# A two-block transformer kernel: Strassen's seven products for half of the second FFN's up projection, in turns of 1024 columns

## The reference

```
# first block, D_FF = 5632
h2 = rmsnorm(x, ffn_norm_g)
x = x + (silu(h2 @ w_ffn_gate) * (h2 @ w_ffn_up)) @ w_ffn_down
# second block, D_FF_2 = 8192
h2 = rms_norm(x, g_ff)
x = x + square(relu(h2 @ w_ff1)) @ w_ff2
```

## Time and profile before

| | us |
|---|---|
| median of 3 runs (lowest, highest) | 2602.14 (2601.84, 2602.91) |
| the profiled execution | 2602.48 |
| its span, first to last instruction | 2600.8 |
| TensorE busy | 2589.1 |
| VectorE busy | 1875.7 |
| ScalarE busy | 1400.5 |
| GpSimd busy | 538.1 |
| FFN 1's steady turns | 717 to 1280 |
| FFN 2 from its second panel | 1923 to 2598 |

### The profile page before, as it was taken

The page is one execution under the profiler, slowest core; times in us unless marked ns, Lnnn a source line. Parts: engine busy times, 40 slices in busy tenths (PEclk is TensorE's granted clock), DMA queues, the critical chain, the costliest instruction groups (busy, mean ns, idle before and its releaser), DMA issues.

```text
span 2600.8 us, 34270 instructions
## 1 busy us (share of the span) xinstructions
PE 2589.1 (100%) x11591; PEld 2153.1 (83%) x11591; DVE 1875.7 (72%) x1944; ACT 1400.5 (54%) x1572; POOL 538.1 (21%) x1034
## 2 busy tenths in 40 slices
PE   9999999999999999999999999999999999999999
PEld 8888888888788888888878888888888888888887
DVE  6767788667888888888986655566666666666666
ACT  5546666445555555566555557764454444444443
POOL 2212121232121222222033120003332121212121
PEclk9999999999999999999999999999999999999999
DMA  8666666766588888888787665566766666666664
GB/s 272 212 201 212 210 219 194 251 218 209 187 248 242 243 246 243 245 245 245 251 269 218 200 200 166 180 206 206 227 217 208 201 208 202 208 202 209 201 210 154
DMA packets 305477, 564.61 MB, mean 217 GB/s; under 512 B 28512, under 2 KB 41872, under 8 KB 304880
## 3 DMA queue, kind: packets, MB, share of 16 engines
q1 hardware_dynamic: 261952, 502.25, 59.1%
q0 software_dynamic: 43264, 61.18, 10.5%
q10 hardware_dynamic: 176, 0.07, 0.0%
HBM read 503.75 MB, written 2.10 MB: 194 GB/s over the span
## 4 chain that ended last, share of the span: by engine, by line
PE 91%; PEld 3%; DVE 2%; issue 1%; DMA 1%; SPq 1%; DVEq 1%; POOL 0%; ACT 0%; ACTq 0%; POOLq 0%
PE pair L2339 20%; PE pair L2334 20%; PE pair L2343 20%; PE aux L2339 4%; PE aux L2334 4%; PE aux L2343 4%; PE pair L2623 4%; PE aux L2623 3%; PE aux L2605 2%; PE aux L2608 2%; PE aux L2602 2%; PEld pair L2334 1%; PEld pair L2339 1%; PEld pair L2343 1%; PE pair L2608 1%
## 5 line engine op out<-in xcount | busy, mean ns | idle before, releaser
L1417 DVE TENSOR_TENSOR w_lo<-raw,w_hi 128x1024 fp32r<-128x1024 f32 (+1 forms) x856 | 1026.2, 1216 | 525.2 <-ACT w_hi L808 512.5
L808 ACT ACTIVATE w_hi<-raw 128x1024 fp32r<-128x1024 f32 (+1 forms) x854 | 893.5, 1055 | 905.0 <-PE pair L2343 637.4
L2334 PE MATMUL pair<-w_hi,lhs_hi 128*128 128x512 f32 x1536 | 414.0, 391 | 0.7 <-ACT lhs_hi L860 0.7
L2339 PE MATMUL pair<-w_hi,lhs_lo 128*128 128x512 f32 x1536 | 411.1, 389 | 1.1 <-DVE lhs_lo L1470 1.0
L2343 PE MATMUL pair<-w_lo,lhs_hi 128*128 128x512 f32 x1536 | 411.1, 389 | 0.0
L729 POOL DMA_DIRECT2D arena<-arena x528 | 263.2, 604 | 713.5 <-DVE arena L1921 598.8
L2339 PEld LDWEIGHTS pair<-w_hi,lhs_lo 128*128 128x128 f32 x1536 | 288.2, 188 | 62.2 <-DVE lhs_lo L1470 1.9
L2343 PEld LDWEIGHTS pair<-w_lo,lhs_hi 128*128 128x128 f32 x1536 | 288.0, 188 | 61.0 <-DVE w_lo L1417 1.1
L2334 PEld LDWEIGHTS pair<-w_hi,lhs_hi 128*128 128x128 f32 x1536 | 286.1, 188 | 59.3 <-ACT lhs_hi L860 1.2
L2334 PE MATMUL pair<-w_hi,low_hi 128*128 128x512 f32 (+1 forms) x1048 | 278.3, 387 | 0.0
L2339 PE MATMUL pair<-w_hi,low_lo 128*128 128x512 f32 (+1 forms) x1048 | 277.0, 386 | 0.0
(11 more groups left out here) (341 smaller groups left out, 2881.7 us busy)
## 6 DMA issues: line engine op xcount, KB each, us to landing
raw<-in_w_ff SPq DMA_DIRECT2D x128, 1024.0 KB, 5.2
...
```

The source lines that it names most:

```text
L808: nc.scalar.activation(w_hi[:, at.slot(p, k), :, 0:width], raw[:, at.raw_slot(p, k), 2 * h:2 * h + 2, 0:width], ACT.Copy).then_inc(hi_read ...
L1417: v.tensor_tensor(w_lo[:, at.slot(p, k), :, 0:n], raw[:, at.raw_slot(p, k), 2 * h:2 * h + 2, 0:n], w_hi[:, at.slot(p, k), :, 0:n].bitcast( ...
L2334: nc.tensor.matmul(ps[:, t, 0:n], hi_t[:, ch, tok], w_hi[:, s, c, 0:n], start=start and k == 0 and c == 0, stop=False)
L2339: nc.tensor.matmul(ps[:, t, 0:n], lo_t[:, ch, tok], w_hi[:, s, c, 0:n], start=False, stop=False)
```

## The change

FFN 2 gets FFN 1's form. `ffn2_first` has two ordinary panels of w_ff1 (columns 0 to 1023). Then come TURNS2 = 7 turns (6 in `ffn2`, one in `ffn2_last`), each with 1024 columns of w_ff1 as eight units, four of them by the seven products, and four down panels of 1024 rows (LONG: 8 chunks, 4 granules). A turn gives two groups of 512 hidden columns, so it has two transposes, two moves and two `hid_turn`s, after unit pairs 2 and 6 of the next turn; the second move waits until the first `hid_turn` has been taken, as `move` and its one buffer demand. The results of the last turn's groups go to buffers of their own (`last_hi`, `last_lo`). Down panels are still added by `add_x`, now after the weights of the panel behind. In FFN 1, `hid_turn` stands after unit pair 4 and not 2, and the `t_used` credit is given ahead of `ffn_first`. `move`, `flip`, `recombine`, `seven` and `ordinary` are used as they are.

```diff
+TURNS1 = NB1 - 1
+TURNS2 = NB2 // 2 - 1
+LONG = (8, N)
-    ("ffn2_first", 1, [FULL]),
-    ("ffn2", NB2 - 2, [FULL] + [SHORT] * 4),
-    ("ffn2_last", 1, [FULL] + [SHORT] * 8),
+    ("ffn2_first", 1, [FULL, FULL]),
+    ("ffn2", TURNS2 - 1, [FULL, FULL] + [LONG] * 4),
+    ("ffn2_last", 1, [FULL, FULL] + [LONG] * 8),
...
+            def load_wide_unit(at, u, col):
+                p, k = unit(u)
+                r = at.raw_slot(p, k)
+                sp.wait_ge(lo_ready, at.gran(p, k) + 2)
+                rows = w_ff1_2[0][2 * u * P:(2 * u + 2) * P, bass.ds(col, 2 * N)]
+                sp.dma_start(raw[:, r].rearrange("p (c w) n -> p c (w n)", w=2),
+                             rows.rearrange("(c p) n -> p c n", p=P)).then_inc(raw_loaded[r], 16)
             def ffn2_block(at, i):
-                load(at, 0, w_ff1_2[0], i * N + N)
+                for u in range(8):
+                    load_wide_unit(at, u, i * (2 * N) + 2 * N)
                 for j in range(4):
-                    load(at, 1 + j, w_ff2_2[0], j * N, i * N)
+                    load(at, 2 + j, w_ff2_2[0], j * N, i * (2 * N))
...
@@ scalar, FFN 1
-                    if u == 2:
+                    if u == 4:
                         hid_turn(i)
@@ scalar, FFN 2
             def block2(at, i, last=False):
+                n = i + TURNS1
+                b = i * 2 + NB1
+                for u in (2, 4, 6):
+                    hi_ordinary(at, u, None)
+                    hi_seven(at, u + 1, None)
+                    hi_sums(u + 1, n)
+                    if u == 2:
+                        hid_turn(b, 0, T_FF2 - 1)
+                    if u == 6:
+                        hid_turn(b + 1, 4, T_FF2 - 1)
+                hi(at, 2, 0, 2)
+                act.wait_ge(products, n * 3 + 1)
+                nc.scalar.activation(first_product, aux[:, 0, :], ACT.Copy).then_inc(product_copied, 1)
+                hi(at, 2, 2, 4)
+                act.wait_ge(gates_ready, n + 1)
+                relu_rows(act_f, [gates[:, 1, :], gates[:, 0, :]], b + 2)
+                hi(at, 3, 0, 1)
+                act.wait_ge(hid_ready, b + 4)
+                relu_rows(gates, [hid[:, 0, :], hid[:, 1, :]], b + 3)
+                hi(at, 3, 1, 4)
+                hi(at, 4, 0, 4)
+                if last:
+                    hid_turn(b + 2, 0, T_FF2 - 1, dst=last_hi)
+                hi(at, 5, 0, 4)
+                if last:
+                    hi(at, 6, 0, 2)
+                    hid_turn(b + 3, 4, T_FF2 - 1, dst=last_hi)
+                    hi(at, 6, 2, 4)
+                else:
+                    nxt = At("ffn2", i + 1)
+                    hi_ordinary(nxt, 0, None)
+                    hi_sums(1, n + 1)
+                    hi_seven(nxt, 1, None)
...
             at = At("ffn2_last")
+            block2(at, TURNS2 - 1, True)
+            for j in range(1, 4):
+                hi(at, 6 + j, 0, 4)
@@ vector, FFN 1
                 unit_pair(at, 2, i)
+                unit_pair(at, 4, i)
                 hid_turn(i)
-                unit_pair(at, 4, i)
@@ vector, FFN 2
+            x_norm(5, 18, lambda: s_forms(At("ffn2_first")))
+            lo(at, 1, 2, 4)
             relu_square(at, NB1, pairs[at.pair(0)][:])
+            lo(at, 1, 4, 6)
+            dve.wait_ge(s_hi_ready, 2)
+            v.tensor_tensor(s_lo[:], s_sum[:], s_hi[:].bitcast(F32), ALU.subtract)
+            dve.drain().then_inc(s_ready, 1)
+            lo(at, 1, 6, 8)
+            sums_seven(first, 1, TURNS1, False)
+            lo_ordinary(first, 0)
+            lo_sums(1, TURNS1)
+            lo_blocks(first, 1)
+            relu_square(at, NB1 + 1, pairs[at.pair(1)][:])
             def block2(at, i, last=False):
+                n = i + TURNS1
+                b = i * 2 + NB1
+                unit_pair(at, 2, n, False)
+                hid_turn(b)
+                unit_pair(at, 4, n, False)
+                unit_pair(at, 6, n, False)
+                hid_turn(b + 1, 4)
+                lo(at, 2, 0, 2)
+                recombine(at, n, 0)
+                lo(at, 2, 2, 4)
+                dve.wait_ge(act_ready, b + 3)
+                for t in range(TOK):
+                    v.scalar_tensor_tensor(act_f[:, t, :], gates[:, 1 - t, :], x_inv[:, t:t + 1],
+                                           act_f[:, t, :], ALU.mult, ALU.mult)
+                dve.drain().then_inc(hid_ready, 1)
+                flip(b + (2 + T_FF2), by_chunk(act_f), n_split=1)
+                lo(at, 3, 0, 1)
+                dve.wait_ge(act_ready, b + 4)
+                for t in range(TOK):
+                    v.scalar_tensor_tensor(hid[:, t, :], hid[:, t, :], x_inv[:, t:t + 1],
+                                           gates[:, t, :], ALU.mult, ALU.mult)
+                dve.drain().then_inc(hid_ready, 1)
+                lo(at, 3, 1, 4)
+                add_x(at, 2, 0)
+                lo(at, 4, 0, 4)
+                add_x(at, 3, N)
+                flip(b + (3 + T_FF2), by_chunk(hid), n_split=1)
+                if last:
+                    hid_turn(b + 2, 0, (last_hi, last_lo))
+                lo(at, 5, 0, 4)
+                add_x(at, 4, 2 * N)
+                if last:
+                    lo(at, 6, 0, 2)
+                    hid_turn(b + 3, 4, (last_hi, last_lo))
+                    lo(at, 6, 2, 4)
+                    add_x(at, 5, 3 * N)
+                else:
+                    nxt = At("ffn2", i + 1)
+                    lo_ordinary(nxt, 0)
+                    sums_seven(nxt, 1, n + 1, False)
+                    lo_sums(1, n + 1)
+                    add_x(at, 5, 3 * N)
+                    lo_blocks(nxt, 1)
...
             for j in range(3):
+                lo(at, 7 + j, 0, 4)
+                add_x(at, 6 + j, j * N)
@@ tensor
+            pe.sem_inc(t_used, 2)
             at = At("ffn_first")
...
-            pe.sem_inc(t_used, 2)
             block(At("ffn", 0), 0, True)
...
+            gemm(at, 1, wide)
+            def block2(at, i, first=False):
+                bank_free(at, 0)
+                ordinary(at, 0)
+                bank_free(at, 1)
+                if first:
+                    pe.wait_ge(s_ready, 2)
+                for u in range(1, 8):
+                    if u in SEVEN:
+                        seven(at, u, i + TURNS1)
+                    else:
+                        ordinary(at, u)
+                pe.wait_ge(moved_taken, i * 2 + (NB1 + T_FF2 + 2))
                 for j in range(4):
+                    gemm(at, 2 + j, low)
...
             pe.wait_ge(moved_taken, NB1 + NB2 + T_FF2)
             for j in range(3):
+                gemm(at, 6 + j, (last_hi, last_lo))
+            bank_free(at, 9)
+            pe.wait_ge(lo_ready, at.gran(9, 3) + 1 + LO_CREDIT)
             for n, (t, c0, c1) in enumerate(TAIL):
+                for ch in range(8):
...
```

More of the change, by code:

```diff
@@ L338, in two_blocks @@
     third = aux[:, 2:4, :]
-    tail_bank = [pairs[1][:, 0, :], pairs[1][:, 1, :], aux[:, 0, :]]
+    last_pair = pairs[At("ffn2_last").pair(9)]
+    tail_bank = [last_pair[:, 0, :], last_pair[:, 1, :], aux[:, 0, :]]
     sem = nc.alloc_semaphore
@@ L1108, in _, with hid_turn @@
             squares_of(3, at, 3)
-            def hid_turn(b, c0=0, first=0, split=False):
+            def hid_turn(b, c0=0, first=0, split=False, dst=low_hi):
                 if split:
@@ L1399, in _, with relu_rows @@
-            with act.Fori(0, NB2 - 2) as i:
+            hi(at, 1, 4, 6)
+            act.wait_ge(s_sums_ready, 2)
+            nc.scalar.activation(s_hi[:], s_sum[:], ACT.Copy).then_inc(s_hi_ready, 1)
+            hi(at, 1, 6, 8)
+            hi_ordinary(first, 0, None)
+            hi_sums(1, TURNS1)
+            hi_seven(first, 1, None)
+            gate_function(at, 1, NB1 + 1, ACT.Relu, pairs[at.pair(1)][:])
+            def relu_rows(dst, src, b):
+                for t in range(TOK):
+                    nc.scalar.activation(dst[:, t, :], src[t], ACT.Relu, scale=x_inv[:, t:t + 1])
+                act.drain().then_inc(act_ready, 1)
@@ L1928, in lo_ordinary, with sums_seven @@
                 lo(at, p, k, k + 2)
-            def sums_seven(at, u, i):
+            def sums_seven(at, u, i, halves=True):
                 p, k = unit(u)
@@ L2029, in _, with s_forms @@
             at, first = At("ffn_first"), At("ffn", 0)
-            def s_forms():
+            def s_forms(at):
                 def pairs_of(lhs):
@@ L2047, in s_forms @@
                 dve.drain().then_inc(s_sums_ready, 1)
-            x_norm(3, 11, s_forms)
+            x_norm(3, 11, lambda: s_forms(At("ffn_first")))
             lo(at, 1, 2, 4)
@@ L2290, in relu_square @@
                 flip(b + T_FF2, by_chunk(hid), n_split=1)
-            x_norm(5, 18)
-            lo(at, 0, 8, 12)
+            first = At("ffn2", 0)
+            x_norm(5, 18, lambda: s_forms(At("ffn2_first")))
+            lo(at, 1, 2, 4)
             relu_square(at, NB1, pairs[at.pair(0)][:])
-            def block2(at, i, last=False):
```

(34 more changed lines are left out.)

69 lines of the change are left out of this document (31 added, 38 removed).

## The result

The changed kernel takes **2583.89 us** (median of 6 runs, 2581.58 to 2585.04) beside 2601.99 of the kernel before (6 runs, 2601.36 to 2604.32): a ratio of 0.9927, 95% interval 0.9916 to 0.9937. Forecast were 2583.0 and "faster". The profiled execution took 2585.04, with a span of 2583.3: 17.5 less than before, where 19.4 were forecast.

A forecast was written before the change was run, and what follows sets the result against it. TensorE's count of 512-column matmuls at 0.2267 us each was taken to bound both FFNs. Terms -19.04 + 0.14 - 4.7 + 1.2 + 0.3 + 2.7 = -19.4 us from 2602.5 gave a forecast of 2583, range 2579 to 2591.

The forecast's parts named there:

- The bound and the 84 matmuls: In FFN 2, TensorE's matmul count sets the time; seven turns save 84 matmuls at 0.2267 us each: -19.04 us.
- FFN 1's first turn: TensorE's four stalls in FFN 1's first turn go through the earlier credit and later hid_turn: -4.7 us, bounds -3.1 and -4.7.
- VectorE and ScalarE keep up: In FFN 2's turns of 84.3 us, VectorE is busy 85% and ScalarE some 44 us, so the load fits.
- The edges: Between FFN 2's turns, unit 1's weights come 0.2 us late at each of 6 edges: +1.2 us, bounds 0 and 7.2.
- rival 2: FFN 2's edges cost the whole addition, 1.2 us each, or landing data holds sums_seven: 2589 us, chance 0.15.
- The moves: In FFN 2's steady turns a move takes 12.65 us, and the second may take 18.5 before it costs anything: 0.
- Rival 3: VectorE holds GpSimd's DMAs, a move lasts 24.3 us and TensorE stands before each first down panel: 2624 us, chance 0.04.
- The last turn's second move: In FFN 2's last turn it leaves half a microsecond of slack before TensorE's down panels: +0.3 us, bounds 0 and 3.
- The tail: Before the last panel TensorE idles for its last granule's w_lo: +2.7 us, bounds 2.5 and 2.9.
- Rival 4: The idle before the last panel drops the clock to 1.2 GHz, doubling the following 11.2 us: 2594 us, chance 0.04.
- The sum: Over the whole kernel, all terms together give -19.4 us, from 2602.5 to 2583.1, forecast as 2583 us.

The follow-up runs named there:

- late_turn: The changed kernel with FFN 2's first hid_turn after unit pair 4 instead of 2: 2637.22 us, ratio 1.0131 to the kernel before.
- After_again: The changed kernel itself, unaltered, run again beside the other experiments: 2583.09 us, ratio 0.9924 to the kernel before.
- ffn2_only: The changed kernel with both of FFN 1's edits (credit, hid_turn place) undone: 2589.49 us, ratio 0.9952 to the kernel before.
- edge_sums_first: The changed kernel with VectorE doing unit 1's sums ahead of unit 0's w_lo in FFN 2's turns: 2581.90 us, ratio 0.9922 to the kernel before.
- eight_products: The changed kernel with one product of each seven in FFN 2 computed and added twice: 2601.90 us, ratio 0.9998 to the kernel before.
- Tail_granules: The changed kernel with TensorE waiting for the last panel's weights granule by granule: 2578.46 us, ratio 0.9908 to the kernel before.
- tail_fill: The changed kernel with ten matmuls of unused result run in the wait before the last panel: 2581.99 us, ratio 0.9923 to the kernel before.
- both: The changed kernel with the last panel's granule-by-granule waits and the sums first at FFN 2's edges: 2577.61 us, ratio 0.9904 to the kernel before.

## Why the prediction was right, step by step

**The bound and the 84 matmuls: right.** -19.04 forecast; put back, the turn shows 2.73 us for 12 of them, and the medians 18.8 (20 like with like). The pace in FFN 2's turns is 0.2267.

**FFN 1's first turn: the stalls went as forecast, their cost and their causes were misread.** All four stalls went. The term was -4.7, the sum of the idle in the rows; by the pace the stalls cost 5.7, and the runs gave 5.6. I had given the first to the credit and the three others to the place of hid_turn. The runs say 4.1 us for each alone and 5.6 for both, because the credit moves the whole chain up (sums, transpose, move) and ScalarE's wait with it: the moved blocks came 4.0 us earlier, where the prediction had 1.7.

**VectorE and ScalarE keep up: right.** 85% and 52% as worked out, and no stall inside a turn. The order at the edge was the tight place, as said.

**The edges: right, and 0.07 us each too small.** 0.27 at six edges, 1.6 us, against 1.2. The bound of 7.2 (rival 2) did not come.

**The moves: right.** GpSimd issued 16 DMAs in 7.80 and 7.81 us beside VectorE's dense stretches. From the start of the issue to ScalarE's copy it took 12.4 us in the last turn (2529.74 - 2517.37), where ScalarE was waiting for it; late_turn shows 13.6. The prediction had 12.65 from the transpose's end. All of it fits into 18.5. Late_turn shows that this margin is real: move the first hid_turn by one unit pair and it is overdrawn by 5 us a turn. Rival 3 is out. The rule that rival 3 leaned on was read too widely. The Trainium skill, "SBUF — State Buffer", section "SBUF: two separate sides", says that GpSimd can't write its descriptors while VectorE runs an operation in a 2-port mode; an operation with two SBUF inputs it calls in the way only of GpSimd operations that read SBUF. During the 7.8 us of the steady move VectorE was busy for 7.34, all of it TENSOR_TENSOR operations with two inputs from SBUF, and the 16 DMAs took their usual time: the trace agrees with the page, and no run here shows a 2-port operation beside a move.

**The last turn's second move: 0 instead of 0.3**, with the 0.3 us of slack that the last fence on the moves shows.

**The tail: the gap right, its consequence missed.** 2.72 us by the pace (2.56 of idle) against 2.7. Rival 4 said that the clock would fall behind it and double all of the 11.2 us that follow; I gave it 0.04, because four stalls of up to 1.64 left the clock at 1.00. Its mechanism happened and its size was wrong: seven matmuls at half pace, 1.5 us, then full clock again. After_again, ffn2_only, edge_sums_first and eight_products show it too, with 1.5 to 1.7 us lost; late_turn has the same gap without it. Tail_granules, tail_fill and both, where the gap is gone, never show it. So the standstill is needed and is not always enough; what decides stays open.

**The sum: right within 1 us, in part by luck.** By the pace the terms are -19.04 + 0.14 - 5.7 + 1.6 + 0 + 2.72 + 1.5 = -18.8, against the forecast's -19.4. The misses partly cancel: FFN 1's stalls gave 1.0 more than forecast and the last move saved its 0.3, while the clock took 1.5 and the edges 0.4. The spans differ by 18.7 with after_again's trace. With the first trace they differ by 17.5; there VectorE is already 1.1 us late ahead of FFN 1's first turn (its first gate product at 646.00, before at 644.90), where the kernels still do the same work.

By medians the forecast is 0.9 us low. The 11 executions of the kernel after spread from 2581.28 to 2585.04. The three with a mean clock of 1.000 are the fastest (2581.3 to 2581.8), the eight with 0.999 take 2583.1 and more. The fall explains 1.5 to 1.7 of the some 2 us between the groups; no fast execution of this kernel was traced. The rest of the spread has another source that stays open: the kernel before spreads over 2.7 us (2601.44 to 2604.09, 27 runs) with every mean clock at 1.000.
